# Three extra matmuls per step on TensorE in the last six steps of the short attention tiles

## The reference

```python
def block(i):
    ...
    score = jnp.einsum("bths,bth->bts", jax.nn.relu(logits), wib * (N_IDX_HEADS ** -0.5))
    score = jnp.where(causal[None], score, -jnp.inf)
    _, idx = lax.top_k(score, topk)          # topk = 256
    ...
    s = jnp.where(valid[:, :, None, :], s, -jnp.inf)
    p = jax.nn.softmax(s, axis=-1).astype(vg.dtype)
    return jnp.einsum("bthk,btkd->bthd", p, vg)
```

## Time and profile before

| what | value |
|---|---|
| median of three runs | 598.59 us |
| the profiled execution | 599.06 us |
| its span, first to last instruction | 597.3 us |
| PE busy | 539.3 us (90%) |
| ACT busy | 388.9 us (65%) |
| DVE busy | 419.9 us (70%) |
| POOL busy | 211.3 us (35%) |
| mean granted TensorE clock | 0.96 |

### The profile page before, as it was taken

One profiled execution on the slowest core, in us unless ns is written; L12 is line 12 of the kernel. 1 busy time (PEld: TensorE's weight loads), 2 busy tenths in 40 slices (PEclk: granted clock), 3 DMA queues, 4 the chain that ended last, 5 costly groups with the idle time before them and its releaser, 6 DMA issues.

```text
span 597.3 us, 8271 instructions
## 1 busy us (share of the span) xinstructions
PE 539.3 (90%) x2756; PEld 447.6 (75%) x2758; DVE 419.9 (70%) x993; ACT 388.9 (65%) x690; POOL 211.3 (35%) x190
## 2 busy tenths in 40 slices
PE   0499988999999999989999866699999999999995
PEld 0477667888687777778888655678898989888874
DVE  4765659888989889998898757464566656664532
ACT  4572724554498898988898675673657566656631
POOL 6522044031436253588464000580412030314222
PEclk9869999999999999999999959679999999999998
DMA  8993094241011112134452160200102010101011
GB/s 304 397 326 102 19 253 165 57 106 36 12 61 36 36 36 52 48 99 120 106 130 82 29 254 1 82 26 1 41 31 72 1 59 13 42 31 71 1 72 70
DMA packets 19658, 51.98 MB, mean 87 GB/s; under 512 B 4128, under 2 KB 5152, under 8 KB 19616
## 3 DMA queue, kind: packets, MB, share of 16 engines
q1 hardware_dynamic: 19616, 51.45, 27.2%
HBM read 37.81 MB, written 4.19 MB: 70 GB/s over the span
## 4 chain that ended last, share of the span: by engine, by line
PE 73%; DVE 10%; ACT 6%; issue 5%; POOL 2%; DMA 2%; SPq 1%; DVEq 0%; POOLq 0%; ACTq 0%
PE pair L1542 28%; PE pair L1683 14%; PE pair L1705 6%; PE pair L1718 5%; PE pair L1511 4%; PE pair L1647 3%; PE pair L1648 2%; PE pair L1619 2%; DVE score_sb L1365 2%; PE pair L1727 2%; PE pair L1610 2%; PE pair L1611 1%; PE pair L1488 1%; PE pair L1743 1%; DVE tie L1299 1%
## 5 line engine op out<-in xcount | busy, mean ns | idle before, releaser
L1450 DVE TENSOR_TENSOR pt_lo<-pair,pt_hi 128x512 fp32r<-128x512 f32 (+3 forms) x96 | 50.5, 554 | 71.5 <-ACT pt_hi L1060 70.9
L955 ACT ACTIVATE bias_sb<-score_sb,tinies 128x1024 bf16<-128x1024 f32 (+2 forms) x93 | 95.7, 1032 | 4.2 <-DVE tinies L1234 3.9
L1542 PE MATMUL pair<-h_hi,w_hi 128*128 128x512 f32 x304 | 97.8, 403 | 0.0
L1542 PE MATMUL pair<-h_lo,w_hi 128*128 128x512 f32 x304 | 93.9, 390 | 0.0
L1542 PE MATMUL pair<-h_hi,w_lo 128*128 128x512 f32 x304 | 93.6, 389 | 0.0
L1220 DVE TENSOR_SCALAR_CACHE_REDUCE bias_sb<-score_sb,tinies 128x640 bf16<-128x640 f32 (+2 forms) x93 | 72.4, 801 | 0.8
L756 POOL TENSOR_SCALAR w_hi<-w_raw 128x1024 fp32r<-128x1024 f32 (+1 forms) x22 | 23.3, 1060 | 136.2 <-DMA w_raw<-in_w_tiles 115.3
L1542 PEld LDWEIGHTS pair<-h_hi,w_hi 128*128 128x128 f32 x304 | 56.3, 188 | 14.7 <-issue 4.6
L1542 PEld LDWEIGHTS pair<-h_lo,w_hi 128*128 128x128 f32 x304 | 57.1, 188 | 12.3
L1542 PEld LDWEIGHTS pair<-h_hi,w_lo 128*128 128x128 f32 x304 | 57.1, 188 | 12.2
L1060 ACT ACTIVATE pt_hi<-pair 128x512 fp32r<-128x512 f32 (+3 forms) x96 | 43.5, 489 | 28.2 <-PE pair L1718 25.9
(11 more groups left out here) (213 smaller groups left out, 1311.8 us busy)
## 6 DMA issues: line engine op xcount, KB each, us to landing
w_raw<-in_w_tiles SPq DMA_DIRECT2D x21, 512.0 KB, 4.0
ada<-in_ada_w SPq DMA_DIRECT2D x16, 512.0 KB, 12.1
x_sb<-in_x SPq DMA_DIRECT2D x8, 512.0 KB, 8.6
ada_g<-in_ada_w SPq DMA_DIRECT2D x8, 512.0 KB, 5.5
qs<-half_hi SPq DMA_DIRECT2D x16, 256.0 KB, 3.8
qs<-half_lo SPq DMA_DIRECT2D x16, 256.0 KB, 4.7
wo_raw<-in_w_out SPq DMA_DIRECT2D x8, 512.0 KB, 7.3
x_res<-in_x SPq DMA_DIRECT2D x8, 512.0 KB, 3.4
```

Source lines behind the costliest of these rows:

```text
L955: nc.scalar.activation(junk[i], score_sb[:, SCORE_OFF[i]:SCORE_OFF[i] + keys_of(i)], ACT.Sign, bias=cand[:, c:c + 1], scale=-1.0, accum_ou ...
L1450: nc.vector.tensor_tensor(pt_lo[:, 4 * b:4 * b + nc4, hh, :], psum[use % 2][:, 0:nc4 * P].rearrange("p (c q) -> p c q", q=P), f32(pt_hi[:, ...
L1542: ins = nc.tensor.matmul(psum[banks[half]][0:width, :], w[b][:, k, 0:width], hh[:, k, half * HALF:(half + 1) * HALF], start=(k == 0 and p ...
```

## The change

In each of the steps 10 to 15, PE issues three more matmuls between the values matmuls (if the step has them) and the transposes. Their weights are the first 128 columns of key_lo, the moving operand is 512 columns of key_hi, and they write bank 7, which the ranking no longer needs by then. Nobody reads the result. So that they don't overwrite a ranking that DVE still reads, PE waits ahead of them for all six masks.

```diff
+WARM_AT = range(10, 16)
+WARM_MATMULS = 3
...
                     ins.then_inc(pv_ps, 1)
+                if g in WARM_AT:
+                    pe.wait_ge(bias_ok, len(PICK))
+                    for _ in range(WARM_MATMULS):
+                        nc.tensor.matmul(psum[7][:, :], key_lo[:, 0:P], key_hi[:, 0:HALF], start=True, stop=True)
                 if LAG_T <= g < 64 + LAG_T:
```

## The result

The changed kernel takes 601.4 us (median of 17 runs, 600.18 to 603.74), the kernel before in the same number of runs 598.13 us. The ratio is 1.0055, with a 95% interval of 1.0039 to 1.0070: about 3.3 us slower. That is the number of the first rival, the clock that falls for a short while, and not that of the forecast. It lies in the range, 597.5 to 602.1 us; the loss is a little more than the 0.5% that was counted as no change, and the interval reaches to both sides of it.

A forecast was written before the change was run, and what follows sets the result against it. Fixed PE work follows piece 0 of the output projection, whose start POOL was to bound. Starting 0.5 us later, against the 598.59 us median, gave 599.1 us; the range was 597.5 to 602.1 us.

The forecast's parts named there:

- the first rival: Clock falls anyway for a short while around steps 10 to 12; piece 0 2.8 us late, 601.4 us; chance 0.28.
- The forecast's case: Clock stays full through the short steps, POOL sets piece 0's start, 0.5 us later; 599.1 us; chance 0.50.
- Part 1, the wait: Step 10: transpose waits for last mask and three matmuls, 3.1 us late; o_sb transposes in step 11 1.6 us late.
- Part 2, POOL: POOL's weight slices run gapless from slice 1, 1.4 us late, so piece 0 can start about 401.15 us, 0.5 us later.
- Part 3: PE's way through steps 12 to 18 at full clock: each pair gains 0.3 us, step 11's 1.4 us lateness shrinks to 0.5.
- The estimate of at most 1.0 us of gain, from POOL: POOL's chain ends only 1.0 us short of being the bound, so no clock brings piece 0 forward by more.

The follow-up runs named there:

- filled_wait: The changed kernel with eight more matmuls into free bank 3 in step 10, ahead of the wait for the last mask; ratio to the kernel before 1.0031.
- bank3: The changed kernel with its extra matmuls into bank 3, free after step 9, without the wait for the masks; ratio to the kernel before 1.0003.
- step10_only: The changed kernel with the wait and three extra matmuls in step 10 only; ratio to the kernel before 1.0029.
- bank3_behind: The changed kernel with the matmuls into bank 3, no mask wait, placed behind transposes and fold in steps 10 to 15; ratio to the kernel before 0.9986.
- wait_only: The changed kernel with only the wait for the six masks and none of the new matmuls; ratio to the kernel before 1.0016.
- bank3_six: The changed kernel with six instead of three extra matmuls per step, into bank 3 and without the mask wait; ratio to the kernel before 1.0041.
- late_only: The changed kernel with three extra matmuls in steps 11 to 15 only, nothing new in step 10; ratio to the kernel before 0.9995.

## Why the prediction's case was wrong, and what of it held

**The forecast's case was the wrong one; the first rival's was right.** The step that failed is the choice that the clock holds. The rival had argued by the busy time: about 1.1 us in the stretch, less than the 1.36 us behind which the clock fell before. The clock fell in both traces of the changed kernel before the three matmuls of step 10 had run. That rival gave 2.8 us at piece 0, a ratio of 1.0047; measured are 2.97 us and 1.0055. That the wait made the pause which let the clock fall so early is shown by filled_wait: same wait, no pause, full clock. I had seen the pause and given this case 0.28.

**That the number lay in the range is no merit of the forecast, and the rival's closeness is in part luck.** The range had been drawn wide enough to hold the first rival. The rival's own terms were 1.6 us by step 10, 1.5 us by steps 11 and 12, and 0.3 us back by the next pair. Measured are 2.46 us, 0.7 us, 0.6 us more lost by the next two pairs, and 0.8 us back only behind step 17. Errors of both signs cancelled to within 0.2 us.

**Part 1, the wait, held in mechanism.** The price of the matmuls at full clock, 0.76 us, was measured as 0.80; the handover was 0.05 instead of 0.15 us. At full clock the o_sb transposes were 1.57 us late in filled_wait, 1.6 forecast. In the changed kernel it was 2.46 us, since matmuls, transpose and fold ran at half clock. So the three matmuls cost 1.45 us there (376.54 to 377.99 us), more than the 1.26 us that had been taken as the bound. The 131 ns that the Trainium skill, "TensorE: Matmul & The Clock Gate", Back-to-back issue gap, gives for such a stream are not borne out: 0.80 us for three is 0.27 us each.

**Part 2, POOL, was half right.** In filled_wait slice 1 of wo_lo came 1.36 us later, 1.4 forecast. But POOL bound nothing. In the changed kernel yr_lo's first half ends at 400.75 + 1.27 = 402.02 us and piece 0 starts at 402.74 us, directly behind PE's own scores. Even in the variants that were fastest some 0.4 us lay between.

**Part 3 had the wrong sign.** It took 2.0 us of PE's links in a pair of steps, halved them, and forecast a gain of 0.3 us per pair. Measured at full clock with three extra matmuls is 4.01 us against 3.71, a loss of 0.3 us. So the lag, which was to shrink, grew from 3.2 us in step 13 to 3.8 us in step 17. A large piece of a pair is ACT's, from pt_hi over exponential and slice to pt_hi; the chain view named PE's links, and ACT was busy until the same moment. ACT in the kernel before, the pair that begins at 383.10 us:

```profile
384.18 0.27 ACT L1060 ACTIVATE pt_hi<-pair 128x128 fp32r<-128x128 f32 x1
...
384.74 1.04 ACT L1107 ACTIVATE wo_hi<-wo_raw 128x1024 fp32r<-128x1024 f32 x1
385.68 0.26 ACT L1060 ACTIVATE pt_hi<-pair 128x128 fp32r<-128x128 f32 x1
```

From pt_hi to pt_hi it is 1.50 us here at half clock and 1.51 us in bank3 at full clock, and from the second pt_hi to the next values matmuls 1.13 us in both. Only the way from the values matmuls to the first pt_hi answers to PE: 1.08 us before, 1.37 us in bank3, since the first three matmuls (0.69 us) add more than the clock saves. That is the 0.3 us. I halved links that had a parallel piece of nearly the same length beside them. A sum of this part does not close either: at 0.3 us per pair, 1.4 us shrinks to 0.8 us by step 15, not to 0.5 us. In turn the full clock gave 0.8 us between PV 17 and PV 19, where I had expected some tenths.

**The sum of the loss**, from the table: 2.46 us at the o_sb transposes (1.1 by the wait, 1.4 by three matmuls, most at half clock), 0.7 us more in steps 11 and 12, 0.6 us by two pairs of steps, and 0.8 us back in steps 17 to 19. That makes 3.0 us. The parts are not additive in themselves: the matmuls of steps 11 to 15 cost 0.1 us less than nothing alone, since the full clock behind them was new, and 1.05 us on top of step10_only, whose execution had the full clock in steps 17 to 19 already.

**No version beats the kernel before beyond doubt.** The matmuls behind transposes and fold, in bank 3, come nearest, with 0.9986 (0.9969 to 1.0004). The estimate of at most 1.0 us of gain, from POOL, was not contradicted by any variant.

What stays open: how often steps 17 to 19 run at full clock in the kernel before, of which there is one trace. Its mean clock over the whole execution, 0.960, is near the 0.961 of the timed runs, but that does not tell where the clock was low. This decides by up to 0.8 us what filling the steps is worth. Open is also which place of the extra matmuls is best: the intervals of bank3 and bank3_behind overlap.

## What to carry to other kernels

Work that is added to fill an idle engine should be ready to run when the engine falls idle: a wait in front of it keeps the pause that it was meant to fill, and everything queued behind it pays. Put it behind what other engines wait for, not ahead; for this half the traces speak (4.44 against 5.05 us in one pair of steps), while the timed runs do not separate the two places. Before counting on a faster clock, look in each loop for a parallel chain of nearly the same length; and compare landmarks from a common event, since spans of single executions differed here by more than the change was worth.

## What the runs showed of the hardware

After PE had fallen idle behind the scores of step 10, the granted clock fell to 1.2 GHz about when the dense matmuls began, and stayed there although PE was then busy for 3.57 of 3.60 us. The first of these three stretches of the changed kernel ends shortly before the matmuls, the second is the microsecond in which they begin, the third the one behind it:

```profile
370.00:376.00 6.00, 2.72 (x23) 2.11 (x20) 3.78 (x12) 0.93 (x4) 0.00 (x0) 1.00 0.00 0
376.00:377.00 1.00, 0.46 (x1) 0.46 (x2) 0.45 (x2) 0.00 (x0) 0.00 (x0) 0.78 0.00 0
377.00:378.00 1.00, 1.00 (x4) 0.60 (x4) 0.00 (x0) 0.00 (x0) 0.00 (x0) 0.50 0.57 102
```

In the second trace of the same kernel the fall came within the pause (0.95 from 370 to 376 us, 0.50 from 377 to 381 us). I had not expected a fall at a pause of 2.1 us with dense work right behind it. It was no accident: wait_only and step10_only, which keep the pause, fell within it too (0.78 from 377 to 378 us, the mask ending at 379.15 us; 0.64 from 376 to 377 us, the mask ending at 377.69 us). With the same pause filled the clock stayed at 2.4 GHz up to 394 us. In the six versions that have extra matmuls without waiting for the mask, in step 10 or in the pause of step 11, it fell 4.8 us behind the mask's end at the earliest, and in bank3 and bank3_six not at all. In the kernel before, and in late_only, it fell 1 and 2 us behind the mask's end, after a pause of 1.94 us. So the clock falls without the new wait as well; the wait brings the fall forward, onto work that everything behind it waits for. Three extra matmuls per step did not hold it in every variant either: it stayed full in bank3 and fell for a while in bank3_behind.
